# The order inside one tile's turn of the first expert pass, on ScalarE and on VectorE

## The chip, the cores and the metric

One Trainium2 chip, one of its cores. The number is the device time of one execution in microseconds (us): the median of three runs of the kernel before is 2675.65 us (2672.65 to 2678.57).

## The reference, cut to what matters

One layer of a hybrid decoder on 256 prompt tokens and 8 single-token samples: a modulated norm, a mixer (convolution, a state-space scan, a gated delta rule), an output projection, and then an expert-retrieval mixer, in which the change lies. For every token and each of 8 heads it picks 16 of 128 x 128 experts, and an expert is one row of `u_tab` and one of `v_tab`:

```python
cv, ci = lax.top_k(cand, K)
eid = i1 * PEER_NKEYS + i2
gate = jax.nn.softmax(cv, axis=-1)
a = jnp.einsum('td,thkd->thk', xb, u_tab[eid])
coef = (gate * jax.nn.gelu(a, approximate=False))
return jnp.einsum('thk,thkd->td', coef, v_tab[eid])
```

## The kernel before

For the prompt nothing is gathered. The kernel runs through all experts, in two passes of 128 tiles, one tile being 128 experts (1 MB of weights). The first pass computes, for tile u, the product of all its experts with all 256 tokens, and GELU of it. A dense matrix of gates, zero where an expert was not chosen, is built beside it. The second pass multiplies GELU by gate and then by `v_tab`. The eight samples do gather their rows, by GpSimd's indirect DMAs.

Products are made from split weights: a weight w is a rounded high part and a low remainder. So a tile of the first pass takes these steps, each engine in its own written order (there is no scheduler; the order of the code is the order of the queue):

1. **The load.** SyncE brings tile u into one of four slots of `wring` (line 443). It waits for the slot's former tile, u - 4, to be subtracted.
2. **The cast** (`high_u`, `high`, line 1075, ScalarE): `whi` of the tile, from `wring`. There are two buffers of `whi`, so the cast of tile u + 1 waits until TensorE has finished tile u - 1.
3. **The subtraction** (`low`, line 1367, VectorE): `wlo` = `wring` - `whi`, after the cast.
4. **The products** (`u_tile`, TensorE): 16 matmuls of 512 columns with `whi`, and then 16 of 256 columns with `wlo`, into PSUM bank u % 2. The first wait for the cast of tile u and for the sum of tile u - 2, which frees the bank; the last 16 wait for the subtraction of tile u.
5. **The half copy** (`half`, line 1287, ScalarE): one half of the bank from PSUM to SBUF (`zh`).
6. **The sum of the halves** (`add_halves`, line 1367 with `ps` as an input, VectorE): `zh` plus the other half, into one of three buffers `z`. It waits for the half copy, and for the store of tile u - 3 out of the same buffer to have landed.
7. **GELU** (`gelu`, line 1292, ScalarE), in place in `z`.
8. **The store** (line 461, SyncE): `z` of tile u to `a_dram`.

A *turn* u is one round of each engine's loop. In turn u ScalarE casts tile u + 1, copies the half of tile u - 1 and does GELU of tile u - 2, and then extras (copies of gates, line 1279). VectorE takes one *piece* of the retrieval (`next(found)`: top-16 searches, one-hot matrices, dot products for the samples), subtracts for tile u + 1, and sums tile u - 1. SyncE in its round u issues the load of tile u + 4, which waits for the subtraction of tile u, and only behind it the store of tile u - 3:

```python
                if n < NE:
                    expert(L_E + n, a["peer_u"][n], n)
                ...
                if u >= 3:
                    e = u - 3
                    sp.wait_ge(sem("gelu_done"), e + 1 + past("gelu_done"))
                    sp.dma_start(a["a_dram"][e // 4, :, ...], z[:, e % 3, :]).then_inc(sem(f"act_stored{e % 3}"), 16)
```

Gates are built for groups of 8 tokens, 32 groups, in every second turn: in the odd turns 31 to 61 and 65 to 95 the piece is `one_hots` (two operations, 128x1024 into bf16). When its first is done GpSimd multiplies one-hots by gates (`gate_rows`, line 2099), and TensorE uses the result two turns later, after its tile (`gate_group`). In the even turns between them the piece is a part of the search for the second half of the tokens (up to turn 58), nothing (turns 64 to 70), or a dot product for one sample (turns 72 to 86). In the turns 87 to 95 GpSimd issues behind `gate_rows` the gather of a sample's rows of `v_tab` (line 2228), which TensorE combines after tiles 88, 90, ... 96 (`combine`, line 908).

Of the kernel before, what the change touches and what calls it, by code (L numbers as in the profile page):

```python
# [123 lines left out]
def build(nc, a, o):  # L124
    with ExitStack() as ctx:
        sem_of = {}

        def sem(name):
            name = REUSED[name][0] if name in REUSED else name
            if name not in sem_of:  # L130
                sem_of[name] = ctx.enter_context(nc.semaphore(name))
            return sem_of[name]

        def past(name):

            return REUSED[name][1]
# [870 lines left out]
        def _(act):  # L1007
# [62 lines left out]
            def high(slot, lands, done):  # L1070

                if done is not None:
                    act.wait_ge(gemm_done, done)
                act.wait_ge(sem(f"w_landed{slot}"), lands)
                act.copy(whi[:, slot % 2], wring[:, slot]).then_inc(sem("hi_ready"), 1)  # L1075
# [169 lines left out]
            def spread(t):  # L1245

                act.wait_ge(sem("cv_sub"), t + 1)
                c = cvv if t else cvv_s[0:64]
                act.activation(c, c, ACT.Exp).then_inc(sem("cv_exp"), 1)

            def finish(t):

                t0, n = TILES[t]
                act.wait_ge(sem("tk_ps"), t + 1)
                for j, v in enumerate((i1T, i2T, gT)):
                    act.copy(v[:, t0:t0 + n], ps[:, 7, j * 128:j * 128 + n]).then_inc(sem("tk_ready"), 1)

            def sample_rows(r):

                act.wait_ge(sem("hs_ps"), r + 1 + past("hs_ps"))  # L1260
                act.copy(hs[:, r * 512:(r + 1) * 512], ps[0:TS, 6, :]).then_inc(sem("hs_ready"), 1)

            def x1_turn(r):

                act.wait_ge(sem("x1t_ps"), r + 1 + past("x1t_ps"))
                act.copy(x1t[:, r // 4, (r % 4) * 512:(r % 4 + 1) * 512], ps[:, 6, :]).then_inc(sem("x1t_ready"), 1)


            def gate_copy(g):

                act.wait_ge(sem("g_ps"), g + 1)
                if g % 4 == 0:
                    act.wait_ge(sem("x1t_ps"), 8 + past("x1t_ps"))
                    act.wait_ge(sem("xs_kept"), 1 + past("xs_kept"))
                    if g:
                        act.wait_ge(sem("g_stored"), 16 * (g // 4) + past("g_stored"))
                for h in range(2):
                    t0 = g % 4 * GT + 4 * h
                    act.copy(stage[:, :, t0:t0 + 4].rearrange("p a t -> p t a"),  # L1279
                             ps[:, 2 + 2 * (g % 2) + h, :].rearrange("p (t a) -> p t a", t=4)).then_inc(sem("g_copied"), 1)  # L1280

            def half(u):

                act.wait_ge(gemm_done, T_U + u + 1)
                if u >= 2:
                    act.wait_ge(sem("z_ready"), u - 1)
                act.copy(zh[:, u % 2, :], ps[:, u % 2, TP:2 * TP]).then_inc(sem("half_ready"), 1)  # L1287

            def gelu(u):

                act.wait_ge(sem("z_ready"), u + 1)
                act.activation(z[:, u % 3, :], z[:, u % 3, :], ACT.Gelu).then_inc(sem("gelu_done"), 1)  # L1292

            def high_u(u):

                high((u + 1) % SLOTS, (T_U + u + 1) // SLOTS * 16 + 16, T_U + u)

            for u in range(NE):
                high_u(u)
                if u >= 1:  # L1300
                    half(u - 1)
                if u >= 2:
                    gelu(u - 2)
                if S_ROWS < u <= S_ROWS + 4:
                    sample_rows(u - S_ROWS - 1)
                for t in range(3):
                    if u == S_SPREAD[t]:
                        spread(t)
                    if u == S_TURN[t] + 1:
                        finish(t)  # L1310
                if S_X1 < u <= S_X1 + 8:
                    x1_turn(u - S_X1 - 1)
                g = GROUP_AT.get(u - 3)
                if g is not None:
                    gate_copy(g)
                if u == S_DOT + 15:
                    act.wait_ge(sem("dots"), TS + past("dots"))
                    act.activation(a_s, a_s, ACT.Gelu).then_inc(sem("dots_gelu"), 1)
                if u == S_COMB + 15:
                    act.wait_ge(sem("comb_done"), TS + past("comb_done"))  # L1320
                    act.copy(rows_s, ps[:, 6, :]).then_inc(sem("rows_s"), 1)
                if u == S_NORM + 1:
                    act.wait_ge(sem("rn_ps"), 1 + past("rn_ps"))
                    act.activation(rn, ps[:, 6, 0:TS], ACT.Sqrt, scale=1.0 / D, bias=epsc[:, 0:1]).then_inc(sem("rn_read"), 1)
                if S_WIDE < u <= S_WIDE + 8:
                    i = u - S_WIDE - 1
                    act.wait_ge(sem("wide_ps"), i + 1 + past("wide_ps"))
                    act.wait_ge(sem("g_stored"), 16 * (TP // TG) + past("g_stored"))
                    dst = g2b if i < 4 else fnwb
                    act.copy(dst[:, i % 4 * 512:(i % 4 + 1) * 512], ps[:, 6 + i % 2, :]).then_inc(sem("wide_ready"), 1)  # L1330
# [29 lines left out]
        def _(dve):  # L1360
# [5 lines left out]
            def tt(out, x, y, op):  # L1366
                return dve.tensor_tensor(out, x, y, op)  # L1367
# [71 lines left out]
            def low(n, slot):  # L1439

                dve.wait_ge(sem("hi_ready"), n + 1)
                tt(wlo[:, slot % 2], wring[:, slot], whi_f[:, slot % 2], ALU.subtract).then_inc(sem("lo_ready"), 1)
# [595 lines left out]
            def add_halves(u):  # L2038

                dve.wait_ge(sem("half_ready"), u + 1 + past("half_ready"))  # L2040
                if u >= 3:
                    dve.wait_ge(sem(f"act_stored{u % 3}"), 16 * (u // 3) + past(f"act_stored{u % 3}"))
                tt(z[:, u % 3, :], zh[:, u % 2, :], ps[:, u % 2, 0:TP], ALU.add).then_inc(sem("z_ready"), 1)

            found = retrieval()
            for u in range(NE):
                next(found, None)
                low(L_E + u + 1, (u + 1) % SLOTS)
                if u >= 1:
                    add_halves(u - 1)  # L2050
            add_halves(NE - 1)

            def low_v(i, v):
# [285 lines left out]
```

## Time and profile before

| | us |
|---|---|
| median of three runs | 2675.65 |
| the profiled execution | 2669.56 |
| its span | 2668.0 |
| TensorE busy | 2379.7 (89%) |
| VectorE busy | 1605.1 (60%) |
| ScalarE busy | 1057.6 (40%) |
| GpSimd busy | 410.4 (15%) |
| TensorE waits for VectorE (line 519) in all | 124.0 |

The first expert pass lies between 1072 and 1933 us of the span. Rows of the timeline give the start, the duration, engine, line and operation with output <- inputs and their sizes, and in brackets how long the engine sat idle before and what ended that. Neighbouring operations of one kind are merged into one row with their count. On VectorE, `fp32r<-128x2048` with two SBUF inputs is the subtraction, `128x1024 bf16` the one-hots, and `sb<-sb,ps ... 128x256` the sum of the halves. "DMA to landing" is the time from the issue of a transfer to the arrival of its last semaphore update.

### The profile page before, as it was taken

To read this page: it belongs to the slowest core of one execution; us is meant where nothing else is said; L and a number is where in the kernel's file an instruction comes from. 1 tells how busy PE (TensorE), PEld (TensorE's weight loads), DVE (VectorE), ACT (ScalarE), POOL (GpSimd) and SP (SyncE) were. 2 spreads that over 40 slices of the span, in tenths; PEclk is the share of its full clock that TensorE was granted. 3 is DMA by queue.
4 is the path that set the end of the run, shared out by engine and by line. 5 is a ranking of instruction groups with operands and counts; after the bars stand their busy time and mean duration, and the time that the engine had idled before them with its cause. 6 is when DMAs were issued, how large, how long until landed. Compare 5 with 4: busy or idle time off the path is not lost.

```text
span 2668.0 us, 37571 instructions
## 1 busy us (share of the span) xinstructions
PE 2379.7 (89%) x14455; PEld 2001.3 (75%) x14455; DVE 1605.1 (60%) x1803; ACT 1057.6 (40%) x1276; POOL 410.4 (15%) x179
## 2 busy tenths in 40 slices
PE   6489999488757959999898989999999999999997
PEld 2189999355545959888777878788888888888885
DVE  0277766533417757767888688645555555555555
ACT  1156687111103333454454544444433333333333
POOL 0000000265411000000444455600000000000000
PEclk9799999799967989999999999999999999999998
DMA  9544543388745734456566698685666666666662
GB/s 379 246 156 174 180 167 142 118 323 302 282 170 221 252 127 170 158 195 213 162 219 211 220 335 290 240 287 180 228 250 232 232 235 235 233 233 233 233 233 109
DMA packets 135238, 587.11 MB, mean 220 GB/s; under 512 B 11708, under 2 KB 61252, under 8 KB 75368
## 3 DMA queue, kind: packets, MB, share of 16 engines
q1 hardware_dynamic: 124928, 530.43, 55.6%
q0 software_dynamic: 10224, 55.51, 5.8%
q8 instruction: 58, 0.95, 0.1%
q14 instruction: 28, 0.23, 0.0%
HBM read 540.08 MB, written 45.80 MB: 220 GB/s over the span
## 4 chain that ended last, share of the span: by engine, by line
PE 78%; DMA 6%; DVE 6%; issue 5%; ACT 3%; POOL 2%; SPq 1%; DVEq 0%; ACTq 0%; POOLq 0%
PE ps L519 75%; DVE sb L1367 4%; DMA sb<-in_w_ada 3%; PE ps L554 2%; ACT sb L1075 1%; POOL sb L2099 1%; DMA sb<-in_peer_v,sb 1%; DMA a_dram<-sb 1%; DVE sb L1373 1%; DVE sb L1370 1%; DMA sb<-rows_dram 0%; SPq L443 0%; PE ps L522 0%; POOL sb L2194 0%; PE ps L908 0%
## 5 line engine op out<-in xcount | busy, mean ns | idle before, releaser
L519 PE MATMUL ps<-sb,sb 128*128 128x512 f32 (+7 forms) x13386 | 2235.1, 328 | 200.5 <-DVE sb L1367 124.0
L519 PEld LDWEIGHTS ps<-sb,sb 128*128 128x128 f32 (+1 forms) x13386 | 1956.7, 187 | 523.7 <-issue 176.8
L1367 DVE TENSOR_TENSOR sb<-sb,sb 128x2048 fp32r<-128x2048 f32 (+13 forms) x652 | 1182.3, 1834 | 625.5 <-ACT sb L1075 599.9
L1075 ACT CAST sb<-sb 128x2048 fp32r<-128x2048 f32 x340 | 647.8, 1906 | 939.6 <-PE ps L519 939.2
L2099 POOL TENSOR_TENSOR sb<-sb,sb 128x1024 f32<-128x1024 f32 (+3 forms) x93 | 320.5, 3456 | 580.9 <-DVE sb L1367 510.2
L554 PE MATMUL ps<-sb,sb 128*32 128x512 f32 x768 | 117.9, 709 | 32.8 <-DMA sb<-in_w_ada 21.8
L1367 DVE TENSOR_TENSOR sb<-sb,ps 128x256 f32<-128x256 f32 (+3 forms) x193 | 92.9, 486 | 87.6 <-PE ps L519 81.7
L1367 DVE TENSOR_TENSOR sb<-ps,sb 128x256 f32<-128x256 f32 (+7 forms) x54 | 18.8, 378 | 160.1 <-PE ps L519 154.5
L1373 DVE SCALAR_TENSOR_TENSOR sb<-sb,sb,sb 128x288 f32<-128x288 f32 (+3 forms) x192 | 86.8, 475 | 22.0 <-DMA sb<-v_dram 4.5
L554 PEld LDWEIGHTS ps<-sb,sb 128*32 128x32 f32 x768 | 18.5, 119 | 81.3 <-DMA sb<-in_w_ada 50.8
L1279 ACT COPY sb<-ps 128x512 f32<-128x512 f32 x64 | 66.6, 1155 | 22.8 <-DMA g_dram<-sb 22.8
L2109 POOL DMA_DIRECT2D rows_dram<-sb x1 | 0.7, 702 | 464.2 <-DVE sb L1491 464.2
L1370 DVE TENSOR_SCALAR sb<-sb,sb 128x288 f32<-128x288 f32 (+3 forms) x101 | 31.7, 354 | 49.8 <-ACT sb L1096 49.5
L1292 ACT ACTIVATE sb<-sb 128x256 f32<-128x256 f32 x128 | 53.6, 419 | 14.2 <-DVE sb L1367 14.1
L1180 ACT COPY sb<-ps 128x512 f32<-128x512 f32 x24 | 14.1, 586 | 103.1 <-PE ps L519 103.1
L1287 ACT COPY sb<-ps 128x256 f32<-128x256 f32 x128 | 46.6, 364 | 3.1 <-PE ps L519 3.1
L1050 ACT COPY sb<-ps 128x512 f32<-128x512 f32 x8 | 4.7, 585 | 81.0 <-PE ps L554 81.0
L1373 DVE SCALAR_TENSOR_TENSOR sb<-ps,sb,sb 128x256 f32 (+1 forms) x24 | 10.2, 438 | 44.0 <-PE ps L519 44.0
L522 PE MATMUL ps<-sb,sb 128*128 128x128 f32 (+3 forms) x133 | 22.0, 305 | 15.3 <-DVEq L1696 14.3
L1094 ACT COPY sb<-ps 128x256 f32<-128x256 f32 x36 | 13.4, 373 | 54.6 <-PE ps L519 54.6
L1243 ACT COPY sb<-ps 128x256 f32<-128x256 f32 x16 | 6.0, 372 | 69.1 <-PE ps L519 69.1
L522 PEld LDWEIGHTS ps<-sb,sb 128*128 128x128 f32 (+3 forms) x133 | 17.5, 155 | 19.7 <-DVEq L1696 14.4
(163 smaller groups left out, 604.1 us busy)
## 6 DMA issues: line engine op xcount, KB each, us to landing
sb<-in_peer_u SPq DMA_DIRECT2D x128, 1024.0 KB, 5.1
sb<-in_peer_v SPq DMA_DIRECT2D x128, 1024.0 KB, 5.2
sb<-in_w_ada SPq DMA_DIRECT2D x96, 1024.0 KB, 7.8
sb<-in_w_in SPq DMA_DIRECT2D x52, 1024.0 KB, 4.7
sb<-in_w_out SPq DMA_DIRECT2D x16, 1024.0 KB, 4.9
sb<-in_w_q SPq DMA_DIRECT2D x16, 1024.0 KB, 4.8
a_dram<-sb SPq DMA_DIRECT2D x128, 128.0 KB, 5.1
g_dram<-sb SPq DMA_DIRECT2D x8, 2048.0 KB, 12.2
```

Of the source, the lines that this page charges most:

```text
L519: return pe.matmul(out, l, r, start=start, stop=stop)
L522: return pe.transpose(out, in_, ident[0:in_.shape[0], 0:in_.shape[0]])
L554: last = pe.matmul(ps[32 * j:32 * j + 32, 6, :], sT[:, 4 * s + j, :], wring[:, s, :, :].rearrange("p (k c) n -> p k (c n)", k=4)[:, j, :], ...
L1075: act.copy(whi[:, slot % 2], wring[:, slot]).then_inc(sem("hi_ready"), 1)
L1180: act.copy(Xb.rearrange("p a t -> p (a t)"), ps[:, 0, :]).then_inc(sem("x_ready"), 1)
L1279: act.copy(stage[:, :, t0:t0 + 4].rearrange("p a t -> p t a"), ps[:, 2 + 2 * (g % 2) + h, :].rearrange("p (t a) -> p t a", t=4)).then_inc( ...
L1287: act.copy(zh[:, u % 2, :], ps[:, u % 2, TP:2 * TP]).then_inc(sem("half_ready"), 1)
L1292: act.activation(z[:, u % 3, :], z[:, u % 3, :], ACT.Gelu).then_inc(sem("gelu_done"), 1)
L1367: return dve.tensor_tensor(out, x, y, op)
L1370: return dve.tensor_scalar(out, x, s1, s2, op0, op1)
L1373: return dve.scalar_tensor_tensor(out=out, in0=x, scalar=s, in1=y, op0=op0, op1=op1)
L2099: return pool.tensor_tensor(out, x, y, op)
```

## The change

In a turn ScalarE copies the half first and casts second. VectorE sums the halves first, then does its piece of the retrieval, and then subtracts.

```diff
             for u in range(NE):
-                high_u(u)
                 if u >= 1:
                     half(u - 1)
+                high_u(u)
                 if u >= 2:
                     gelu(u - 2)
...
             for u in range(NE):
+                if u >= 1:
+                    add_halves(u - 1)
                 next(found, None)
                 low(L_E + u + 1, (u + 1) % SLOTS)
-                if u >= 1:
-                    add_halves(u - 1)
             add_halves(NE - 1)
```

VectorE before, turns 33 to 35: `sb_73` is `wlo`, `sb_138` is `z`, `sb_176` is `zh`, `sb_180` and `sb_136` are the one-hots. `hi_ready` tells of the cast, `m_sub`, `m_exp` and `w_exp` of the store that frees the buffer of `z`, `tt_ps` of the half copy.

```order
L1367 TENSOR_TENSOR sb_180<-sb_52,sb_171 128x1024 [waits g_ps]
L1367 TENSOR_TENSOR sb_136<-sb_52,sb_170 128x1024
L1367 TENSOR_TENSOR sb_73<-sb_49,sb_72 128x2048 [waits hi_ready]
L1367 TENSOR_TENSOR sb_138<-sb_176,ps 128x256 [waits m_sub,tt_ps]
L1859 MAX_INDEX sb_163<-sb_162,sb_156 128x8
L1860 MATCH_REPLACE sb_155<-sb_162,sb_156 128x256
L1859 MAX_INDEX sb_163<-sb_162,sb_156 128x8
L1860 MATCH_REPLACE sb_155<-sb_162,sb_156 128x256
L1367 TENSOR_TENSOR sb_73<-sb_49,sb_72 128x2048 [waits hi_ready,dve_steps]
L1367 TENSOR_TENSOR sb_138<-sb_176,ps 128x256 [waits m_exp,tt_ps]
```

VectorE after the change, at the same place:

```order
L1367 TENSOR_TENSOR sb_138<-sb_176,ps 128x256 [waits m_sub,tt_ps]
L1367 TENSOR_TENSOR sb_180<-sb_52,sb_171 128x1024 [waits g_ps]
L1367 TENSOR_TENSOR sb_136<-sb_52,sb_170 128x1024
L1367 TENSOR_TENSOR sb_73<-sb_49,sb_72 128x2048 [waits hi_ready]
L1367 TENSOR_TENSOR sb_138<-sb_176,ps 128x256 [waits m_exp,tt_ps]
L1859 MAX_INDEX sb_163<-sb_162,sb_156 128x8
L1860 MATCH_REPLACE sb_155<-sb_162,sb_156 128x256
L1859 MAX_INDEX sb_163<-sb_162,sb_156 128x8
L1860 MATCH_REPLACE sb_155<-sb_162,sb_156 128x256
L1367 TENSOR_TENSOR sb_73<-sb_49,sb_72 128x2048 [waits hi_ready,dve_steps]
```

As a row of operations this looks the same, and one operation has moved by a turn: before, the sum that follows a subtraction for tile u + 1 is that of tile u - 1; now it is that of tile u. So in the queue there is one subtraction fewer between the subtraction for a tile and the tile's own sum.

ScalarE, turns 8 to 10 of the same loop, before (`sb_72` is `whi`, `sb_176` is `zh`, `sb_138` is `z`, `sb_152` a transposed copy of the tokens):

```order
L1075 CAST sb_72<-sb_49 128x2048 [waits w_landed2,gemm_done]
L1287 COPY sb_176<-ps 128x256 [waits z_ready,gemm_done]
L1292 ACTIVATE sb_138<-sb_138 128x256 [waits z_ready]
L1266 COPY sb_152<-ps 128x512 [waits smp_exp]
L1075 CAST sb_72<-sb_49 128x2048 [waits w_landed3,gemm_done]
```

And after:

```order
L1287 COPY sb_176<-ps 128x256 [waits z_ready,gemm_done]
L1075 CAST sb_72<-sb_49 128x2048 [waits w_landed2,gemm_done]
L1292 ACTIVATE sb_138<-sb_138 128x256 [waits z_ready]
L1266 COPY sb_152<-ps 128x512 [waits smp_exp]
L1287 COPY sb_176<-ps 128x256 [waits z_ready,gemm_done]
```

Cast and copy have changed places; both wait for the end of the same tile. TensorE, GpSimd and SyncE issue what they issued, in the same order.

## Rows read from the trace of the kernel before

**Rows 1.** Waits of TensorE, 1250 to 1740 us: us in total, times, longest

```profile
PE ps L519 <- DVE sb L1367: 38.0, 25, 3.6
```

**Rows 2.** Busy time of each engine in the two stretches with gate groups

```profile
1268.56:1498.52 229.96, 208.53 (x1391) 182.36 (x1391) 196.28 (x156) 114.03 (x132) 94.45 (x16) 0.97 0.60 193
1511.06:1747.15 236.09, 213.61 (x1427) 182.37 (x1428) 177.75 (x114) 109.99 (x127) 138.56 (x39) 0.97 0.82 295
```

**Rows 3.** Timeline, a pair of turns with a search piece

```profile
1299.70 0.41 DVE L1367 TENSOR_TENSOR sb<-sb,ps 128x256 f32<-128x256 f32 x1
...
1301.72 2.29 DVE L1367 TENSOR_TENSOR sb<-sb,sb 128x2048 fp32r<-128x2048 f32 x1
1303.93 0.41 DVE L1367 TENSOR_TENSOR sb<-sb,ps 128x256 f32<-128x256 f32 x1
...
1313.86 0.41 DVE L1367 TENSOR_TENSOR sb<-sb,ps 128x256 f32<-128x256 f32 x1
```

**Rows 4.** Timeline, turns 64 to 68

```profile
1502.69 0.42 DVE L1367 TENSOR_TENSOR sb<-sb,ps 128x256 f32<-128x256 f32 x1
...
1503.02 2.36 DVE L1367 TENSOR_TENSOR sb<-sb,sb 128x1024 bf16<-128x1024 f32 x2
...
1504.39 6.16 POOL L2099 TENSOR_TENSOR sb<-sb,sb 128x3072 bf16<-128x3072 bf16 x1 [19.87 <-DVE sb L1367]
1505.54 1.90 ACT L1075 CAST sb<-sb 128x2048 fp32r<-128x2048 f32 x1 [2.51 <-PE ps L519]
1507.34 0.36 ACT L1287 COPY sb<-ps 128x256 f32<-128x256 f32 x1
1507.47 5.23 DVE L1367 TENSOR_TENSOR sb<-sb,sb 128x2048 fp32r<-128x2048 f32 x1 [2.09 <-ACT sb L1075]
...
1512.62 0.41 DVE L1367 TENSOR_TENSOR sb<-sb,ps 128x256 f32<-128x256 f32 x1
...
1513.18 17.06 PE L519 MATMUL ps<-sb,sb 128*128 128x512 f32 x109 [2.12 <-DVE sb L1367]
...
1526.52 2.29 DVE L1367 TENSOR_TENSOR sb<-sb,sb 128x2048 fp32r<-128x2048 f32 x1 [0.95 <-ACT sb L1075]
...
1528.84 0.34 SPq L443 DMA_DIRECT2D sb<-in_peer_u  x1
...
1529.22 0.54 SPq L461 DMA_DIRECT2D a_dram<-sb  x1
```

**Rows 5.** Stores to a_dram issued in 1240:1500, 1500:1600, 1600:1700 and 1933:1936

```profile
DMA to landing us min/median/max: 5.0/5.2/7.2
DMA to landing us min/median/max: 5.0/7.4/13.5
DMA to landing us min/median/max: 5.0/8.4/8.7
DMA to landing us min/median/max: 1.9/1.9/1.9
```

**Rows 6.** Two stretches: one whole tile, and its 16 matmuls with the high part

```profile
1892.26:1897.82 5.56, 5.56 (x35) 4.88 (x34) 2.63 (x2) 2.49 (x3) 0.00 (x0) 1.00 0.63 212
1892.26:1895.94 3.68, 3.68 (x19) 3.00 (x17) 1.55 (x1) 2.49 (x3) 0.00 (x0) 1.00 0.76 295
```

**Rows 7.** Groups by form, first expert pass: busy us, mean ns

```profile
L2099 POOL TENSOR_TENSOR sb<-sb,sb 128x3072 bf16<-128x3072 bf16 x32 | 199.1, 6222 | 510.6 <-DVE sb L1367 510.0
L519 PE MATMUL ps<-sb,sb 128*128 128x128 bf16 x768 | 48.4, 219 | 0.0
```

**Rows 8.** Timeline, turn 87 and the end of tile 86

```profile
1660.23 2.35 DVE L1367 TENSOR_TENSOR sb<-sb,sb 128x1024 bf16<-128x1024 f32 x2
...
1661.54 1.91 ACT L1075 CAST sb<-sb 128x2048 fp32r<-128x2048 f32 x1 [3.50 <-PE ps L519]
```

**Rows 9.** Gathers for the combine: queue, count, us from issue to landing

```profile
sb<-in_peer_v,sb POOLq DMA_INDIRECT x8, 11.1
```

**Rows 10.** TensorE's waits in the combine, 1511.06 to 1747.15 us

```profile
PE ps L908 <- DMA sb<-in_peer_v,sb: 5.9, 3, 2.9
```

## Prediction

> **What bounds the kernel now.** I read the first pass by itself, since only its turns are changed. Of TensorE's waits there, 38.0 us in 25 pieces were ended by VectorE [rows 1]. That is the most that a better order could give back. Then I asked how much time the turns take beside what TensorE needs. A tile needs 5.56 us [rows 6], a gate group 48.4/32 = 1.51 us [rows 7], so a pair of turns with one group needs 2 x 5.56 + 1.51 = 12.63 us. The 16 pairs of the first stretch took 229.96/16 = 14.37 us each, and those of the second 236.09/16 = 14.76 us [rows 2]. So in the gate stretches TensorE is not the bound.
>
> The timeline tells who is [rows 4]. In an odd turn VectorE makes the one-hots at 1503.02; GpSimd begins its multiplication at 1504.39, 1.37 us later, and runs 6.16 us (mean 6.22 [rows 7]), to 1510.55. The subtraction begins meanwhile, at 1507.47, and takes 5.23 us instead of the 2.29 us of the one at 1526.52. It ends at 1512.70, 2.15 us after GpSimd: it does next to nothing until GpSimd is done. The sum follows at 1512.62, and TensorE, idle for 2.12 us, starts its tile 0.15 us after that sum. So before the change a tile's start hangs on the subtraction (of the next tile) and on the lock on it, though it needs only the sum behind it.
>
> A pair of turns is then a closed chain on VectorE: one-hots to GpSimd 1.37, GpSimd 6.22, rest of the subtraction 2.15, sum 0.33 less an overlap of 0.08, the search piece, a free subtraction 2.21 net (1303.93 - 1301.72 [rows 3]), sum 0.33: 12.53 us and the piece. In [rows 3] the piece is 1301.72 - 1300.03 = 1.69 (it starts 0.33 after the sum at 1299.70, as the one-hots at 1503.02 do after the sum at 1502.69 [rows 4]), which gives 14.22; between the sums at 1299.70 and 1313.86 there are 14.16 us. VectorE is saturated there, its idle time covered by GpSimd's lock.
>
> **The change part by part.** *ScalarE.* The copy comes 0.36 us after the end of a tile instead of 1.80 + 0.36, and the cast's end moves from 1.9 to 1.9 + 0.28 = 2.2 us [rows 4]. The tile that needs the cast starts 5.56 us after that end: covered, costs nothing. If the cover went it would be 0.28 us in each of 128 turns, 36 us.
>
> *VectorE, the sum first.* A tile's start now needs neither the subtraction nor the piece. The subtraction is due only 3.68 us into its tile [rows 6]. So VectorE may run 3.68 + 0.41 = 4.1 us further behind before TensorE stalls. In the saturated stretches this is won once each, up to 2 x 4.1 us; single waits like that of 2.12 us go. But a saturated chain has the same operations as before, so its pace is not better. I cost the gain at 0 to -11 us, and take 0, since the next step makes the chain longer and uses up the room again in a pair or two.
>
> *The store that frees the buffer of z.* This is the step that decides. The sum of tile u waits for the store of tile u - 3. SyncE issues that store only behind the load of tile u + 4, which waits for the subtraction of tile u. Before, between the subtraction of tile u and the sum of tile u stood a sum, a piece, the subtraction u + 1, a sum, a piece and the subtraction u + 2. Now the last sum, piece and subtraction have gone from between them. The store is issued 1529.22 - 1528.81 = 0.41 us after the end of the subtraction [rows 4], and lands 5.2 us later in the median [rows 5]; with 0.1 us for the release (an estimate; other releases in [rows 4] take 0.03 to 0.15) the sum can start 5.71 us after the end of the subtraction of its tile number. Meanwhile VectorE has, in the even turns of a pair, only the previous sum, a piece and one free subtraction: 0.33 + 1.69 + 2.21 - 0.08 = 4.15 us. It waits about 1.56 us there, with a dot product of 2.3 us about 1.0, and with no piece at all (turns 64 to 70, 88 to 94) about 3.2. Behind the waiting sum are queued the one-hots, hence GpSimd, and the subtraction that TensorE's next tile needs. In odd turns GpSimd's lock is longer than the store and hides it; in the turns without gate groups VectorE is idle anyway and the store lands at about 0.41 + 5.2 + 4.6 = 10.2 us after the end of tile u - 2, with the sum due at 2 x 5.56 + 0.4 = 11.5. So turns 2 to 30 and 97 to 127 cost nothing.
>
> A pair with a gate group becomes: store 0.41 + 5.2 + 0.1, sum 0.33, one-hots 1.37, GpSimd 6.22, rest 2.15 = 15.78 us, whatever the piece. TensorE's 12.63 stay below it.
> First stretch: 16 x 15.78 = 252.5, less 229.96: **+22.5 us**.
> Second stretch: stores there land in 7.4 to 8.4 us in the median, with a minimum of 5.0 [rows 5], since gathers share the engines. The store that counts is the one behind the locked subtraction; a sample's two transfers are issued after the dot product, thus behind it, and are mostly over a pair later. So I take 6.0, nearer to the lower end: 16 x 16.58 = 265.3, less 236.09: **+29.2 us**. Bounds: 5.2 gives +16.4, 8.4 gives 16 x 18.98 - 236.09 = +67.6.
>
> *The gathers.* The one-hots of turn 87 began at 1660.23, about 1.3 us before tile 86 ended, the end that released the cast at 1661.54 [rows 8]. Now they come behind half copy and sum, 0.36 + 0.41 and releases = about 0.9 us after it. From there 1.37 + 6.22 + 0.15 + 11.1 [rows 9] = 18.8 us to landed rows, against 12.6 us until TensorE wants them: 7.1 us of wait, for about three of the five combines 87 to 95 (a wait puts the next one off), 19 against the 5.9 before [rows 10]: +13. The slower pairs absorb half or more: **+6**, between 0 and 13.
>
> Sum: 22.5 + 29.2 + 6 = +57.7 us. On the profiled 2669.56 that is 2727.3. The median of the runs lies 6.09 above the profiled time, so about 2733.4.
>
> **A rule of the Trainium skill.** It stands apart from the sum. "DMA: Bandwidth & Descriptors", section "Anatomy of one DMA", gives a transfer about 2.0 us and its bytes over 436 GB/s; for the 128 KB of a store that would be an estimate of 2.3 us, and the store would never bind (the first rival). The trace has such a time only for the last store, 1.9 us, and 5.0 as the least for those behind a 1 MB load [rows 5]; the page's section on queues, that an engine takes descriptors in the order of the ring, agrees with the latter.
>
> **The rivals.** *Store never late.* If the store lands in 2 to 4 us after the change, the chain has its old length and only the gathers' +13 stays: 2669.56 + 13 + 6.1 = 2689. Against it: no store behind a load landed below 5.0.
> *Faster.* The mechanism is the earlier start of tiles: VectorE may be 4.1 us later, in the two stretches, and some 3 us of single waits vanish: -11, thus 2665; were VectorE not saturated, all of 38.0, thus 2638. It decides if the store lands within 4.1 us of the subtraction and the one-hots come no later against TensorE. For it speaks that every wait in [rows 1] stands behind a sum, against it the saturated chain of [rows 3].
> *Stores late everywhere.* With 8.4 us in the second stretch and 6 to 13 for the gathers: 22.5 + 67.6 + 6 = +96, 2772; with 7.4, 16 x 17.98 - 236.09 = +51.6 and +80, 2756. For it speak the medians of [rows 5].
> *No difference*, effects that cancel: 2676.
>
> **How the numbers follow.** The forecast, 2712 to 2748, has 0.62; stores late everywhere 0.17; store never late 0.10; faster 0.06; no difference 0.05. Predicted is 2733. The range goes down to 2690, so that half of the store's rival is in it, and up to 2768: left out are 0.06 + 0.05 + 0.05 + 0.03. About 0.2% (5.4 us) is what a measurement here tells from nothing: faster 0.06, within 0.05, slower 0.89.
>
> **What would show it.** Right: VectorE's sums wait for the DMA to `a_dram` some 16 x 1.5 + 16 x 2.5, about 55 us in all; TensorE's waits move from the start of a tile to its middle, before the 256-column matmuls; a sum-to-sum pair in the first stretch lasts 15.8 us; the stretches take about 252 and 270 us; turns 2 to 30 and the second pass are unchanged. Wrong: no such waits for stores, pairs of 14.2 us, or a clear rise of combine waits alone. If stores land in 8 us between 1500 and 1800, the size of the second term is wrong, not the step.

## The result, and the profile after

| | before | after |
|---|---|---|
| median of the runs, us | 2674.15 (4 runs, 2672.15 to 2678.57) | 2742.27 (4 runs, 2735.57 to 2744.22) |
| ratio to before | | 1.0251, 95% interval 1.0230 to 1.0272 |
| profiled execution / its span, us | 2669.56 / 2668.0 | 2743.65 / 2742.1 |
| first stretch (end of tile 31 to end of tile 63), us | 229.96 | 251.38 |
| second stretch (end of tile 65 to end of tile 97), us | 236.09 | 279.51 |

The change made the kernel 2.5% slower: 68 us by the medians. The forecast was 2733 in a range of 2690 to 2768.

Where the time went is read from the same two stretches as in [rows 2], cut at the same tile ends. The columns are: stretch and its length, busy time (and instructions) of TensorE, its weight loads, VectorE, ScalarE and GpSimd, granted clock as a share of TensorE's full clock, DMA share, GB/s.

```profile
1277.06:1528.44 251.38, 215.81 (x1390) 186.89 (x1390) 224.72 (x155) 112.36 (x132) 96.18 (x16) 0.95 0.55 174
1540.98:1820.49 279.51, 231.06 (x1427) 193.88 (x1427) 217.06 (x113) 108.79 (x127) 140.51 (x40) 0.90 0.69 252
```

They are 21.4 and 43.4 us longer, 64.8 in all. What lies outside differs by 8.5 us ahead of the first tile (1081.0 after, 1072.5 before, in code that the change does not touch; in the runs below this start lies anywhere between 1069.3 and 1081.1). Turns 2 to 31 take the same, turns 97 to 127 take 184.25 against 184.19, the second pass is within a microsecond.

The granted clock is lower too, 0.95 and 0.90 where both stretches had 0.97, and TensorE is busy 7.3 and 17.5 us longer with the same number of matmuls. In these stretches it sits idle for 35.6 and 48.5 us, where it sat idle for 21.4 and 22.5. No run tells how much of the loss the clock makes by itself, but the pairs below are accounted for without it: the longer times lie in a chain of VectorE, GpSimd and a store, of which TensorE is no part but in one pair and at the end of the second stretch.

Who waits for whom in the first stretch (us in total, times, longest), after the change:

```profile
PE ps L519 <- DVE sb L1367: 35.6, 15, 4.3
DVE sb L1367 <- DMA a_dram<-sb: 25.4, 16, 3.8
```

and in the second:

```profile
DVE sb L1367 <- DMA a_dram<-sb: 48.3, 15, 9.1
PE ps L519 <- DVE sb L1367: 32.9, 13, 5.6
ACT sb L1279 <- DMA g_dram<-sb: 22.4, 2, 12.5
```

VectorE waits for a store to `a_dram` once in each of the 16 pairs, 25.4/16 = 1.59 us at a time. Before, it waited so three times in the whole program, 3.3 us together. TensorE's waits for VectorE are 35.6 us in the first stretch alone, against 38.0 in both [rows 1].

The stores themselves did not become slower. Those issued in 1240:1500 and in 1600:1700 of after:

```profile
DMA to landing us min/median/max: 4.9/5.1/8.1
DMA to landing us min/median/max: 5.0/5.7/13.3
```

One pair shows the mechanism. The subtraction that runs while GpSimd multiplies, and stands still until GpSimd is done, is called the locked one here. The timeline of after, a pair with a search piece (start, us, engine, line, operation; in brackets the idle time before it and who ended it):

```profile
1305.85 7.41 DVE L1367 TENSOR_TENSOR sb<-sb,sb 128x2048 fp32r<-128x2048 f32 x1
...
1313.18 0.41 DVE L1367 TENSOR_TENSOR sb<-sb,ps 128x256 f32<-128x256 f32 x1
1313.29 0.33 SPq L443 DMA_DIRECT2D sb<-in_peer_u  x1
...
1313.31 12.84 PE L519 MATMUL ps<-sb,sb 128*128 128x256 f32 x88 [1.28 <-DVE sb L1367]
...
1313.66 0.44 SPq L461 DMA_DIRECT2D a_dram<-sb  x1
...
1315.21 2.29 DVE L1367 TENSOR_TENSOR sb<-sb,sb 128x2048 fp32r<-128x2048 f32 x1
...
1318.72 0.42 DVE L1367 TENSOR_TENSOR sb<-sb,ps 128x256 f32<-128x256 f32 x1 [1.22 <-DMA a_dram<-sb]
1319.06 9.67 DVE L1367 TENSOR_TENSOR sb<-sb,sb 128x1024 bf16<-128x1024 f32 x3
1320.36 6.23 POOL L2099 TENSOR_TENSOR sb<-sb,sb 128x3072 bf16<-128x3072 bf16 x1 [9.25 <-DVE sb L1367]
```

The locked subtraction ends at 1305.85 + 7.41 = 1313.26. SyncE issues first the load that waited for it, then at 1313.66 the store, 0.40 us after the subtraction. The store lands 5.0 us later, and the sum starts 0.1 us behind that, at 1318.72, 5.46 us after the subtraction; VectorE had had nothing to do for 1.22 us. Behind the sum stand the two one-hots and the next locked subtraction (one row, x3), which ends at 1328.73. From 1313.26 to there it is 15.47 us, where before the change a pair with a piece took 14.16. TensorE goes on at 1313.31 after a wait of 1.28 us, now in the middle of a tile: its first matmuls after the wait are those with 256 columns, which need the subtraction; in [rows 4] it waited at the start of a tile, for the sum.

On the chain that ended last, the page puts 6% on the stores to `a_dram`, and 15% on VectorE:

```profile
PE 68%; DVE 15%; DMA 11%; issue 2%; POOL 1%; ACT 1%; SPq 1%; DVEq 0%; ACTq 0%; POOLq 0%
```

From the end of one locked subtraction to the end of the next, the steps are the same in nearly every pair of both stretches: 0.41 us to the issue of the store, its landing, 0.09 to the sum, 1.64 to GpSimd's start, 8.38 to the end of the locked subtraction. So a pair is 10.5 us and the landing, and the landing alone makes most of the difference between pairs: 4.97 us in the one above and 6.84 in the next, which takes 17.35. Over 15 pairs the landing is 5.37 us on average in the first stretch and 6.04 in the second.

In the second stretch nine of 15 pairs take 15.5 to 16.1 us, one 17.1, and the last three 18.0 to 18.4. Two stand out, with 23.9 and 20.9 us. The timeline of the first:

```profile
1616.02 0.43 SPq L468 DMA_DIRECT2D g_dram<-sb  x1
...
1625.89 4.01 SPq L443 DMA_DIRECT2D sb<-in_peer_u  x1
...
1629.94 0.64 SPq L461 DMA_DIRECT2D a_dram<-sb  x1
...
1633.23 2.03 ACT L1279 COPY sb<-ps 128x512 f32<-128x512 f32 x2 [12.55 <-DMA g_dram<-sb]
...
1637.47 0.36 ACT L1287 COPY sb<-ps 128x256 f32<-128x256 f32 x1
...
1639.72 0.42 DVE L1367 TENSOR_TENSOR sb<-sb,ps 128x256 f32<-128x256 f32 x1 [9.11 <-DMA a_dram<-sb]
```

The 2 MB of gates stored at 1616.02 hold up two things. ScalarE's gate copy waits for that store until 1633.23, and the half copies queue behind it, so the half that the sum at 1639.72 needs is there only at 1637.83. And the issue of the next load takes 4.01 us instead of 0.33, so the store of `z` behind it leaves at 1629.94, 4.08 us after the subtraction, and lands 9.7 us later. Either of the two alone would have put off the sum. The pair at 1686 to 1707 has the same picture: an issue of 3.71 us, a gate copy that waits 9.88 us. Before the change the load behind such a store took as long to issue, 4.50 us at 1581.03 and 4.67 at 1640.58, and the pairs there took 15.5 and 14.7: no sum was waiting for the store behind it.

In the first stretch gate copies wait too (5.6, 8.1 and 5.6 us), but every sum of an even tile there is released by its store: the half is there before it.

### The profile page after: what moved, and what is told of

Read it like the earlier page. It is cut to its first block, busy times and chain, and to the rows that moved or that the text cites. A ratio compares the mean times of both kernels' runs of the same rounds, so it can differ in the third digit from the quotient of the medians.

```text
span 2742.1 us, 37571 instructions
## 1 busy us (share of the span) xinstructions
PE 2411.4 (88%) x14455; PEld 2022.3 (74%) x14455; DVE 1673.9 (61%) x1803; ACT 1054.7 (38%) x1276; POOL 409.6 (15%) x179
## 4 chain that ended last, share of the span: by engine, by line
PE 68%; DVE 15%; DMA 11%; issue 2%; POOL 1%; ACT 1%; SPq 1%; DVEq 0%; ACTq 0%; POOLq 0%
PE ps L519 65%; DVE sb L1367 13%; DMA a_dram<-sb 6%; DMA sb<-in_w_ada 3%; PE ps L554 2%; POOL sb L2099 1%; DMA sb<-in_peer_v,sb 1%; DVE sb L1373 1%; SPq L443 1%; DVE sb L1370 1%; DMA sb<-rows_dram 0%; PE ps L522 0%; POOL sb L2194 0%; DMA sb<-in_state_gdn 0%; ACT sb L1350 0%
## 5 line engine op out<-in xcount | busy, mean ns | idle before, releaser
L519 PE MATMUL ps<-sb,sb 128*128 128x512 f32 (+7 forms) x13386 | 2263.4, 331 | 229.3 <-DVE sb L1367 153.3
L519 PEld LDWEIGHTS ps<-sb,sb 128*128 128x128 f32 (+1 forms) x13386 | 1977.3, 190 | 562.6 <-issue 146.5
L1367 DVE TENSOR_TENSOR sb<-sb,sb 128x2048 fp32r<-128x2048 f32 (+13 forms) x652 | 1243.6, 1932 | 429.1 <-ACT sb L1075 401.2
L554 PE MATMUL ps<-sb,sb 128*32 128x512 f32 x768 | 119.4, 717 | 36.9 <-DMA sb<-in_w_ada 25.4
L1367 DVE TENSOR_TENSOR sb<-ps,sb 128x256 f32<-128x256 f32 (+7 forms) x54 | 18.8, 379 | 167.9 <-PE ps L519 162.3
L522 PEld LDWEIGHTS ps<-sb,sb 128*128 128x128 f32 (+3 forms) x133 | 17.8, 156 | 19.7 <-DVEq L1696 14.4
```

Of the source, the lines that this page charges most:

```text
L519: return pe.matmul(out, l, r, start=start, stop=stop)
L522: return pe.transpose(out, in_, ident[0:in_.shape[0], 0:in_.shape[0]])
L554: last = pe.matmul(ps[32 * j:32 * j + 32, 6, :], sT[:, 4 * s + j, :], wring[:, s, :, :].rearrange("p (k c) n -> p k (c n)", k=4)[:, j, :], ...
```

## Experiments

The theory: the pace is set by the store that frees the buffer of `z`, which is issued behind a load, which waits for the subtraction. The main rival: the order on ScalarE and VectorE costs the time by itself, in the wait for the half or the lag of the subtraction, and the stores are only what is seen waiting. The table gives the medians, the ratio to before with its 95% interval, and from the profiled execution the two stretches and turns 97 to 127, in us. Before has 229.96, 236.09 and 184.2 there, after 251.38, 279.51 and 184.3.

| run | median | ratio | first | second | 97 to 127 |
|---|---|---|---|---|---|
| e1 after, store ahead of load | 2697.18 | 1.0104 (1.0072 to 1.0136) | 229.8 | 261.3 | 185.9 |
| e2 before, store a round later | 2748.84 | 1.0293 (1.0269 to 1.0317) | 254.1 | 276.5 | 189.8 |
| e3 ScalarE's part alone | 2675.77 | 1.0017 (1.0003 to 1.0032) | 230.5 | 240.4 | 186.1 |
| e4 VectorE's part alone | 2755.34 | 1.0316 (1.0288 to 1.0344) | 255.6 | 285.9 | 184.3 |
| e5 e1, gate store ahead of both | 2694.80 | 1.0104 (1.0074 to 1.0134) | 226.1 | 258.4 | 185.9 |
| e6 e5, combine two turns later | 2671.59 | 0.9998 (0.9980 to 1.0016) | 226.0 | 236.6 | 183.8 |
| e7 before, piece beside the lock | 2668.39 | 0.9995 (0.9979 to 1.0012) | 221.4 | 237.2 | 184.3 |
| e8 all of these | 2648.51 | 0.9918 (0.9888 to 0.9947) | 212.4 | 220.1 | 187.8 |
| e9 after, piece behind the subtraction | 2706.38 | 1.0136 (1.0112 to 1.0159) | 225.0 | 267.8 | 183.3 |
| e10 before, combine two turns later | 2665.73 | 0.9980 (0.9963 to 0.9998) | 229.9 | 228.3 | 187.1 |

### e1: the store ahead of the load

```diff
                 n = u + SLOTS
-                if n < NE:
-                    expert(L_E + n, ...)
...
                 if u >= 3:
                     e = u - 3
                     sp.wait_ge(sem("gelu_done"), ...)
                     sp.dma_start(a["a_dram"]..., z[:, e % 3, :])
+                if n < NE:
+                    expert(L_E + n, ...)
```

> The changed kernel, but SyncE issues the store of tile u - 3 ahead of the load of tile u + 4, so the store no longer waits for the subtraction of tile u. Theory (a sum waits for a store that stands behind that load): VectorE's waits for a_dram in the first pass, 82 us after the change, fall below 10 us; pairs of turns with a gate group go from 15.7 back to about 14.2 us in the first stretch; only later gathers remain of the loss: 2687 us (2675 to 2700). Rival (the one-hots come later against TensorE, behind the sum, and GpSimd's lock then holds the subtraction that TensorE needs next): the store is a bystander and the time stays at 2730 to 2745.

Measured 2697.18. No sum waits for a store any more, and the first stretch is back at 229.8 us, where before had 230.0: its whole loss is gone with the store's wait, though both new orders stand. A pair of it in the timeline:

```profile
1306.75 0.41 DVE L1367 TENSOR_TENSOR sb<-sb,ps 128x256 f32<-128x256 f32 x1
...
1307.08 9.67 DVE L1367 TENSOR_TENSOR sb<-sb,sb 128x1024 bf16<-128x1024 f32 x3
1307.35 0.34 SPq L457 DMA_DIRECT2D a_dram<-sb  x1
```

The sum comes with the subtraction before it (1304.54, 2.29 us), not 1.2 us later. The median is 10 us above the value expected, inside its range. The second stretch keeps 25 us of its 43, and they lie in two places: the two pairs at a gate store take 20.1 and 20.0 us where the pairs around them take 14.7, and the combine waits 14 us longer than before. The next runs try both. That stretch's waits:

```profile
DVE sb L1367 <- ACT sb L1287: 30.0, 8, 6.0
ACT sb L1279 <- DMA g_dram<-sb: 21.9, 3, 10.8
...
PE ps L908 <- DMA sb<-in_peer_v,sb: 19.9, 3, 7.2
```

The combine waits three times, 19.9 us. Gate copies wait for the store of gates, and sums for half copies, some of which stand behind those gate copies on ScalarE.

### e2: the late store without the change

```diff
-            for u in range(NE + 3):
+            for u in range(NE + 4):
...
-                if u >= 3:
-                    e = u - 3
+                if u >= 4:
+                    e = u - 4
```

> The kernel before, with both orders as they were; SyncE issues each store one round later, so in the queue one subtraction fewer lies between the issue of the store of tile u - 3 and the sum of tile u, as after the change. Store theory: the same wait appears without the change: pairs of the first stretch about 15.7 us, time 2715 to 2745. Rival (order of the one-hots and the lock): the sums have slack to spare and the time stays within 2669 to 2682.

Measured 2748.84, a little above the range. ScalarE's and VectorE's orders are those of before; only SyncE's store comes one load later. The loss is there, in the same places: 254.1 and 276.5 us.

```profile
1307.74 0.33 SPq L443 DMA_DIRECT2D sb<-in_peer_u  x1
1308.12 0.43 SPq L461 DMA_DIRECT2D a_dram<-sb  x1
1310.63 0.42 DVE L1367 TENSOR_TENSOR sb<-sb,ps 128x256 f32<-128x256 f32 x1 [2.91 <-DMA a_dram<-sb]
1310.96 9.67 DVE L1367 TENSOR_TENSOR sb<-sb,sb 128x1024 bf16<-128x1024 f32 x3
```

Here the sum is released by the store issued at 1303.88, just behind the locked subtraction that ended at 1303.47; it landed 6.7 us later. The next such sum comes at 1326.21: a pair of 15.6 us. The steps of a pair are those of after, 10.5 us and the landing. With e1 this shows the cause from both sides: the wait alone makes the loss, and without the wait the first stretch has none. The excess over the expectation lies partly in turns 97 to 127, which are 5.6 us longer, and in turns 2 to 31, 1.9 us longer.

### e3 and e4: one part at a time

e3 takes ScalarE's part of the diff alone (half, then cast), e4 VectorE's alone.

> Only ScalarE's part of the change: half copy, then cast. Store theory: VectorE's queue is as before, the subtraction begins 0.28 us later in turns without a lock and a tile's start follows it: 2674 to 2681. Rival (the later cast is what TensorE waits for): 128 turns x 0.28 = 36 us, so about 2710.

> Only VectorE's part: the sum, then the piece, then the subtraction, with the half copy still behind the cast. Store theory: all of the loss is here, and the half copy that comes 1.8 us later adds little in stretches bound by the store: 2740 (2730 to 2765). Rival (the loss needs both parts, since the cast is late): 2674 to 2710.

e3: 2675.77, ratio 1.0017; the first stretch is that of before (230.5), the second 4.3 us longer. So ScalarE's part by itself is all but free. e4: 2755.34, and that is above after itself (1.0316 against 1.0251, intervals apart; 13 us between the profiled executions). VectorE's part makes the whole loss, and ScalarE's part takes some of it back. In e4 the half comes behind the cast, 1.9 us later, and the sum that has been moved up waits for it: VectorE waits for half copies 50.3 us, and for stores only 48.9, between 1250 and 1830 us, where after has 22.5 and 75.4.

```profile
DVE sb L1367 <- ACT sb L1287: 50.3, 21, 6.5
DVE sb L1367 <- DMA a_dram<-sb: 48.9, 21, 8.8
```

### e5 and e6: what was left of the second stretch

```diff
 # e5, on e1: in SyncE's loop
+                g = GROUP_AT.get(u - 4)
+                if g is not None and g % 4 == 3:
+                    ... store of 2 MB to g_dram, ahead of the store of z and the load
 # e6, on e5
-S_DOT, S_COMB, S_BACK, S_NORM, S_WIDE = 72, 88, 104, 106, 110
+S_DOT, S_COMB, S_BACK, S_NORM, S_WIDE = 72, 90, 106, 108, 112
```

> The changed kernel with the store of z ahead of the load (as in e1_store_first, 2697 us) and the store of the gates (g_dram, 2 MB, every eighth turn) ahead of both. What e1 still loses against the kernel before is in the second stretch, 261.3 us against 236.1. Theory A: two pairs of turns there last 21.5 us since ScalarE's gate copy waits 10.8 us for the gate store to land, and that store too stands behind a load that waits for the subtraction; it goes out earlier now, these two pairs go to 14 to 17 us, and the time is about 2686 us (2680 to 2692). Theory B: the waits come from transfers that share the engines, not from the place in the queue: 2697 stays.

> As e5_gate_store_first, and TensorE's combines of the samples start two turns later (after tiles 90 to 104 instead of 88 to 102; what follows them moves by two turns as well). Theory: in e1 three combines waited 19.9 us for gathered rows since the one-hots, GpSimd's multiplication and so the gather come later against TensorE; with two turns more all of that goes, 15 to 20 us less than e5: about 2670 us. Rival: the gathers wait for earlier combines, so the wait only moves: within 5 us of e5.

e5: 2694.80 does not decide by its time: it lies nearer to the rival's value than to the theory's. The stretches are 3.7 and 2.9 us shorter than in e1, and the waits of gate copies for `g_dram` in the second fall from 21.9 to 14.7 us. The two pairs at the gate stores, from locked subtraction to locked subtraction, were 23.9 and 20.9 us in after and 20.1 and 20.0 in e1; here they are 18.6 and 19.2, above the 14 to 17 that theory A wanted. So the place of the gate store is worth a few microseconds, not ten. e6 is clear: 2671.59 where about 2670 was expected. Giving the gathers two turns more takes 21.8 us from e5's second stretch, and its TensorE waits nowhere for rows of `peer_v`. With the stores early and the gathers in time, the order of the change is as fast as the kernel before, and no faster. Its long pairs at the gate stores are still there (18.7 and 19.0 us).

### e10: the later combine by itself

```diff
-S_DOT, S_COMB, S_BACK, S_NORM, S_WIDE = 72, 88, 104, 106, 110
+S_DOT, S_COMB, S_BACK, S_NORM, S_WIDE = 72, 90, 106, 108, 112
```

> The kernel before, combines two turns later and nothing else. Combine waits there are 5.9 us, so the gain is 3 to 7 us: 2667 to 2671. So of what the kernel with all changes gains (23 us) this part is at most 7.

Measured 2665.73, ratio 0.9980. On the kernel before the same edit takes 7.8 us from the second stretch, against 21.8 on e5, and gives 2.9 back in turns 97 to 127. So the 21.8 in e6 are mostly what the change had added: the one-hots, and with them the gathers, had come later. e10 is also the fairer measure for e6, since both have the later combine: e6's first stretch is 3.9 us shorter (226.0) and its second 8.3 us longer (236.6), and the two ratios, 0.9998 and 0.9980, are not apart by their intervals.

### e7: the search piece beside the lock

The pair of turns is a chain on VectorE, and the subtraction does next to nothing while GpSimd multiplies. The search piece could run there instead, if it doesn't need the port.

```diff
                     if u in GROUP_AT:
                         one_hots(GROUP_AT[u])
-                    elif u <= 58:
-                        next(two)
+                        if u <= 57:
+                            next(two)
```

> The kernel before with both orders as they were; the search piece of each even turn 32 to 58 is done one turn earlier, right behind the one-hots, while GpSimd holds VectorE's subtraction back. Theory (a closed chain on VectorE of 12.5 us and the piece bounds the first stretch): the piece leaves the chain, pairs go from 14.4 to TensorE's 12.6 us, the first stretch from 230 to about 206 us, the time to about 2650 us (2645 to 2656). Rival (pieces with two SBUF inputs are held back by GpSimd as the subtraction is): 2668 to 2680.

The median is 2668.39, ratio 0.9995: a miss in size. The first stretch fell by 8.6 us, not by 24. This search piece does run at its full speed under the lock:

```profile
1317.51 2.35 DVE L1367 TENSOR_TENSOR sb<-sb,sb 128x1024 bf16<-128x1024 f32 x2
...
1318.81 6.23 POOL L2099 TENSOR_TENSOR sb<-sb,sb 128x3072 bf16<-128x3072 bf16 x1 [7.27 <-DVE sb L1367]
1319.78 1.40 DVE L1865 MAX8 sb<-sb 128x8 f32<-128x256 f32 x4
...
1322.03 5.15 DVE L1367 TENSOR_TENSOR sb<-sb,sb 128x2048 fp32r<-128x2048 f32 x1 [0.85 <-ACT sb L1075]
...
1327.66 4.52 PE L519 MATMUL ps<-sb,sb 128*128 128x512 f32 x21 [0.76 <-DVE sb L1367]
```

Four MAX8 in 1.40 us, 0.35 each, while GpSimd multiplies from 1318.81 to 1325.04; the subtraction meanwhile ends 2.14 us after GpSimd, as ever. But of the 15 pairs of this stretch, from multiplication to multiplication, only three take the 12.4 to 12.6 us that TensorE needs; the others take 12.9 to 15.2.

Part of the reason is that the run's rival was right for some pieces. Four of the 14 are an operation with two inputs in SBUF (128x2048, 2.28 us in the kernel before). Under the lock each takes 7.41 us, as the subtraction does, and the subtraction comes behind it. One row holds such a turn: both one-hots, the piece, the subtraction.

```profile
1400.67 12.00 DVE L1367 TENSOR_TENSOR sb<-sb,sb 128x1024 bf16<-128x1024 f32 x4
```

The pairs behind these four are 14.8 to 15.2 us, so moving them gained nothing: 2.2 to 2.6 us each over 12.5, some 10 of the 21 us by which the stretch exceeds 16 x 12.5. Two operations with a single input are held as well: a COPY of 128x8 takes 5.28 us where it took 0.16, and a TENSOR_SCALAR of 128x128 takes 3.03 where it took 0.23. FIND_INDEX8, MATCH_REPLACE8 and TENSOR_REDUCE (128x2048, 2.27 us) take the same with and without the lock. In the order of before a tile's start still stands behind the locked subtraction too; the other pairs were not taken apart.

### e9: sum, subtraction, piece

```diff
 # on after
                     add_halves(u - 1)
-                next(found, None)
                 low(L_E + u + 1, (u + 1) % SLOTS)
+                next(found, None)
```

> The changed kernel with one more exchange on VectorE: sum, then subtraction, then piece of the retrieval; SyncE and the combines as in the kernel before. Store theory: between the subtraction for a tile and the tile's sum there stand two pieces again, one of them the one-hots, 0.33 + 2.21 + 1.69 + 2.35 = 6.6 us against the 5.7 a store needs, so no sum of the first stretch waits for a store, and with the sum under the lock the chain is 12.1 us and the piece = 13.8: first stretch 215 to 226 us. The one-hots come 4 us later against TensorE than in the changed kernel, so combines wait 20 to 35 us: time 2675 to 2695. Rival (any order with the sum first loses): 2720 or more.

The expectation held for the length of the first stretch (225.0 us) and failed for the whole: 2706.38. A piece behind the subtraction lets the next load and the store go 1.7 us earlier, and the sums' waits for stores fall from 25.4 to 6.4 us there, though not to nothing as expected. The second stretch is what went wrong, 267.8 us: the combine waits 14.2, 8.8 and 8.5 us, since the one-hots now stand behind the subtraction as well.

```profile
PE ps L908 <- DMA sb<-in_peer_v,sb: 31.6, 3, 14.2
ACT sb L1279 <- DMA g_dram<-sb: 29.0, 3, 14.1
```

The first stretch agrees with the store's wait a third way. That the one-hots come still later is read from the combine's waits, not tried by itself.

### e8: all of it

The orders of the change with the piece behind the subtraction (e9), the stores ahead of the load (e5), the piece beside the lock (e7), the combine later (e6).

> ScalarE: half copy, then cast. VectorE: sum, then subtraction, then piece, and in the turns 31 to 57 one-hots and search piece together. SyncE: gate store, store of z, load. Combines two turns later. Theory: no tile waits at its start for a subtraction, no sum for a store, the search pieces lie under GpSimd's lock; what is left are the dot products, 8 pairs of about 14.5 us: first stretch about 203 us, second about 222, time 2632 us (2622 to 2645). Rival: subtraction ahead of the one-hots makes GpSimd start late and the lock fall on the subtraction of the next turn, which TensorE needs earlier: 2660 or more.

Measured 2648.51, ratio 0.9918 (0.9888 to 0.9947): 0.8% faster than before and 3.2% than after, yet 16 us above what was expected. The two stretches:

```profile
1273.26:1485.67 212.41, 204.41 (x1390) 179.70 (x1390) 205.75 (x156) 112.52 (x132) 99.61 (x16) 0.98 0.59 207
1498.21:1718.29 220.08, 209.38 (x1420) 180.42 (x1419) 192.01 (x114) 109.51 (x127) 134.99 (x40) 0.97 0.85 306
```

From tile end to tile end 13 of the 32 pairs take 12.5 us, TensorE's own time; 16 such pairs are 200. For the stretches 203 and 222 were expected: they make 7.5 of the 16 us, and turns 97 to 127, longer than before by 3.6, some more. The first stretch is 9.4 us above its 203, and the four pieces that GpSimd holds back account for 9: they take 7.40 to 7.41 us here too, and each makes a pair of 14.8 us, from multiplication to multiplication, instead of 12.5. The expectation had all search pieces hidden under the lock. In the second stretch, which came 2 us below its 222, two pairs are the largest, 18.8 and 19.7 us. The pair of 18.8, in the timeline:

```profile
1551.91 9.78 SPq L462 DMA_DIRECT2D a_dram<-sb  x1
...
1561.73 0.43 SPq L443 DMA_DIRECT2D sb<-in_peer_u  x1
...
1562.21 0.59 SPq L462 DMA_DIRECT2D a_dram<-sb  x1
...
1569.76 0.42 DVE L1367 TENSOR_TENSOR sb<-sb,ps 128x256 f32<-128x256 f32 x1 [5.11 <-DMA a_dram<-sb]
...
1570.32 14.93 PE L519 MATMUL ps<-sb,sb 128*128 128x512 f32 x86 [3.60 <-DVE sb L1367]
```

At 1551.48 the 2 MB of gates were stored; the issue of the small store behind them takes 9.78 us, the load and the next small stores go only then, and the sum waits 5.11 us. So the gate store is what is left of the stores, and putting it ahead of the others (e5) makes it stand in their way.

The order of the change costs nothing that these runs can tell once the stores and the gathers are out of its way (e6). Whether it pays was not separated: the whole gives 23 us by the medians, while e7 and e10 alone give 3 and 6, and e7's interval contains no change. The rest comes from the parts together, the order among them.

## Why the prediction was right, point by point

**What bounds the kernel: held.** VectorE's chain sets the pair. When the store's wait was put in it the stretches grew, by the change (251.4) and without it (e2, 254.1).

**ScalarE, taken at 0: held within a few microseconds, but not independent.** Alone it costs 4.5 us by the ratio (1.0017, the interval from 0.8 to 8.6 us). With VectorE's part it is worth some 17 us to the better (1.0316 to 1.0251), which the prediction did not see: it costed the earlier half copy only by what the later cast could spoil, not by what the earlier sum needs.

**VectorE's room of 4.1 us, taken at 0: held.** With stores and gathers out of the way (e6) the ratio is 0.9998; against e10, which has the later combine as well, no gain shows either.

**The store: held, in place and size.** In the pair shown the issue comes 0.40 us behind the subtraction (0.41 forecast) and the sum 5.46 us behind it (5.71); the wait is 1.59 us per pair (1.56). The first stretch grew by 21.4 us where 22.5 was forecast. It is the step that decides, and e1 and e2 show it.

**The second stretch: right step, one term missing.** The forecast had +29.2 for stores landing in 6.0 us and +6 for gathers, +35.2; it was +43.4. The landings that count average 6.04 us over the 15 pairs, and 16 pairs of 10.52 + 6.04 are 265.0 us (265.3 forecast), +28.9. So the term for stores held. No row gave the 6.0, it was chosen between 5.2 and 8.4, and that it came so near is in part luck: without the two pairs at a gate store the average is 5.68. The missing term is the late issue: in those two pairs the 2 MB store of gates keeps SyncE in the issue of the load for 4.01 and 3.71 us, so that the store of `z` behind it leaves 3.7 and 3.4 us late, +7.1. The prediction put gate stores at nothing without a reason, though the two slow issues were in the trace of before. What is left is some 7.5 us, and it lies where TensorE waits for gathers (+6 forecast): in one pair (18.4 us) the sum waited 2.25 us beyond the landing, for the half of a tile that a combine had put off, and the end of the stretch, with the last combine's wait in it, is 5.3 us longer than a pair; that end was not taken apart. TensorE waited 15.6 us in five combines where it had waited 5.9 in three [rows 10], that is 9.7 more, where 13 more was forecast. The prediction's own sum for these waits has a slip: three waits of 7.1 us are 21, not 19.

**The waits as a test.** About 55 us for stores were forecast in the stretches, though the product that stands beside it, 16 x 1.5 + 16 x 2.5, is 64; 25.4 + 48.3 = 73.7 were found. Single waits of 9.1 and 6.2 us, of the two long pairs, make most of the surplus. TensorE's waits moved to the middle of tiles, and turns 2 to 30 and the second pass stayed, as said.

**The total.** 57.7 forecast, 64.8 found in the stretches. With the later start of 8.5 us the profiled execution was 74 us longer; the medians differ by 68, and 2742 lies 9 above the forecast and inside its range.

**The rule of the Trainium skill.** "DMA: Bandwidth & Descriptors", section "Anatomy of one DMA", would let a store of 128 KB land in an estimated 2.3 us; it gives its figures for transfers that GpSimd issues, and this store goes out on SyncE. No store behind a load in the two stretches landed below 4.9 in either kernel, so by the measurement that rule does not carry to a store queued behind 1 MB. "SBUF — State Buffer", section "SBUF: two separate sides", says of the port pair that VectorE and GpSimd share that whoever starts first has it for the whole instruction, and that on VectorE's side this holds for an operation with two inputs in SBUF or in a mode that uses both of its ports. The trace agrees for two inputs: the subtraction that takes 2.29 us alone takes 7.41 beside a multiplication of 6.23, and the search's MAX8 with one SBUF input does not notice it (e7).

## What to carry to other kernels

When an operation is moved up in a queue, look for what its buffer waits for: the store that frees it may be issued behind a load that hangs on the very operation it was moved past. Put small stores that free a buffer ahead of large loads on an issuing queue, and check what large store stands ahead of them. Before hiding work beside GpSimd, look at each operation's time there: in e7 some ran at full speed and others stood still. Of two parts of a change ask also what each is worth when the other is there: here one cost nothing alone and saved 17 us beside the other.

## What the runs showed of the hardware that was not expected

The issue of a DMA can itself take long. SyncE's issue takes 0.33 to 0.44 us in most rows. Behind a 2 MB store to `g_dram` it took 5.3 to 5.5 us in the first stretch of e8 and 7.9 to 11.5 in the second, and most in e5 (14.15) and in e1:

```profile
1638.77 0.43 SPq L468 DMA_DIRECT2D g_dram<-sb  x1
1639.25 13.69 SPq L457 DMA_DIRECT2D a_dram<-sb  x1
1652.98 1.50 SPq L443 DMA_DIRECT2D sb<-in_peer_u  x1
```

Everything behind it on that queue waits too. In after the next issue came about 10 us behind the gate store: in the first stretch it took 0.34 us, at 1625.89 and 1696.51 it took 4.01 and 3.71; at 1767.45, 12 us behind, 0.34 again. So it ends when the large store is far enough on: in e8 all eight such issues ended 2.6 to 3.4 us before the 2 MB store landed, whether that took 8.9 us or 14.8. What it waits for exactly was not found.

Under GpSimd's multiplication VectorE's MAX8 ran at 0.35 us each and its sum, with one operand in PSUM, at 0.41 to 0.42, as without it, while the subtraction with two inputs in SBUF stood still until GpSimd was done. A COPY and a TENSOR_SCALAR with one input in SBUF stood still too (e7), so the number of inputs alone does not tell.

A fourth buffer of `z`, which should take the wait away without moving any instruction, was not tried.
